# The S5 output products of a decoder trunk: one burst a round over four column groups, in place of four separate calls

## The reference

```
lam_bar = exp(lam * dt)
bu    = einsum('blgh,gph->blgp', ug, b_bar)          # complex
state = linear_scan(broadcast(lam_bar), bu)          # over the 256 tokens
y     = einsum('blgp,ghp->blgh', state, c_c).real + d * ug
```

## Time and profile before

| | |
|---|---|
| median of 3 runs | 2974.36 us (2973.3 to 2975.58) |
| profiled execution, its own time | 2973.05 us |
| its span, first to last instruction | 2971.0 us |
| mean granted TensorE clock | 0.993 |
| TensorE busy | 2894.8 us, 97% |
| VectorE busy | 2010.5 us, 68% |
| ScalarE busy | 1582.0 us, 53% |
| GpSimd busy | 751.4 us, 25% |

### The profile page before, as it was taken

How to read it: one execution, slowest core, us unless ns; L and a number is a source line. 1 busy time by engine, 2 the same in 40 slices (tenths; PEclk the granted TensorE clock), 3 DMA queues, 4 the chain that set the end, 5 groups by cost and what they waited for, 6 DMA issues and landing times.

```text
span 2971.0 us, 56245 instructions
## 1 busy us (share of the span) xinstructions
PE 2894.8 (97%) x16280; PEld 2454.7 (83%) x16280; DVE 2010.5 (68%) x3316; ACT 1582.0 (53%) x2828; POOL 751.4 (25%) x813
## 2 busy tenths in 40 slices
PE   6999999999999999999989999999999999999997
PEld 5878888888888888888877788888888888888886
DVE  7788888755555667555568888887555555665555
ACT  5555554565555655444455554546555655644443
POOL 3145445401000123111123544543000011221110
PEclk9999999999999999999999999999999999999998
DMA  6655555655555556777745555555555555577775
GB/s 225 213 174 159 162 159 154 170 170 168 159 158 164 165 156 195 209 214 209 206 142 174 167 162 159 159 162 171 171 157 164 160 168 154 158 213 209 215 209 176
DMA packets 276414, 522.69 MB, mean 176 GB/s; under 512 B 30912, under 2 KB 33872, under 8 KB 275280
## 3 DMA queue, kind: packets, MB, share of 16 engines
q1 hardware_dynamic: 257360, 477.13, 54.8%
q10 hardware_dynamic: 18944, 44.18, 4.5%
HBM read 508.60 MB, written 16.78 MB: 177 GB/s over the span
## 4 chain that ended last, share of the span: by engine, by line
PE 46%; DVE 2%; issue 2%; ACT 1%; DVEq 0%; POOL 0%; ACTq 0%; POOLq 0%
PE ps L294 26%; PE ps L293 13%; PE ps L443 1%; PE ps L337 1%; DVE w L975 1%; PE ps L456 0%; PE ps L452 0%; PE ps L296 0%; PE ps L325 0%; PE ps L338 0%; DVE zb L1523 0%; PE ps L326 0%; PE ps L327 0%; PE ps L304 0%; PE ps L313 0%
## 5 line engine op out<-in xcount | busy, mean ns | idle before, releaser
L294 PE MATMUL ps<-hb,w 128*128 128x512 f32 x5824 | 2059.1, 396 | 7.3 <-POOL hb L1553 6.1
L975 DVE TENSOR_TENSOR w<-raw,w 128x512 fp32r<-128x512 f32 x1760 | 1290.2, 738 | 859.5 <-ACT w L590 845.1
L590 ACT ACTIVATE w<-raw 128x512 fp32r<-128x512 f32 x1760 | 1098.2, 629 | 1138.6 <-PE ps L294 1135.9
L293 PE MATMUL ps<-hb,w 128*128 128x256 f32 x5690 | 1632.4, 287 | 13.2 <-DVE w L975 11.8
L294 PEld LDWEIGHTS ps<-hb,w 128*128 128x128 f32 x5824 | 1092.9, 188 | 250.5 <-issue 6.7
L293 PEld LDWEIGHTS ps<-hb,w 128*128 128x128 f32 x5690 | 1076.0, 189 | 70.8 <-issue 29.3
L294 PE MATMUL ps<-gl,w 128*128 128x512 f32 x640 | 226.6, 395 | 0.0
L1576 POOL TENSOR_TENSOR xx<-g,tab 128x512 f32<-128x512 f32 x64 | 121.0, 1891 | 269.6 <-DVE g L1038 269.1
L1703 POOL TENSOR_TENSOR nf<-zb 128x256 f32 (+1 forms) x60 | 51.9, 864 | 537.1 <-DVE zb L1491 531.6
L294 PE MATMUL ps<-w,hb 128*128 128x512 f32 x512 | 180.8, 395 | 0.0
L293 PE MATMUL ps<-gl,w 128*128 128x256 f32 x560 | 156.6, 280 | 0.0
(11 more groups left out here) (296 smaller groups left out, 2582.1 us busy)
## 6 DMA issues: line engine op xcount, KB each, us to landing
raw<-in_w SPq DMA_DIRECT2D x1763, 256.0 KB, 2.8
mlaw<-in_mlaw ACTq DMA_DIRECT2D x16, 768.0 KB, 4.2
mlaw<-in_mlaw ACTq DMA_DIRECT2D x16, 512.0 KB, 3.5
gate<-xres ACTq DMA_DIRECT2D x32, 256.0 KB, 4.5
xres<-zb ACTq DMA_DIRECT2D x32, 256.0 KB, 3.7
zb<-in_x SPq DMA_DIRECT2D x8, 512.0 KB, 7.5
xres<-in_x SPq DMA_DIRECT2D x4, 1024.0 KB, 7.0
s5w<-in_s5w ACTq DMA_DIRECT2D x16, 256.0 KB, 3.5
```

Source lines behind the costliest of these rows:

```text
L293: mm(acc[:, T:], a_lo, m_hi, start=False, stop=False, skip_group_check=True)
L294: last = mm(acc, a_hi, m_both, start=(k == 0), stop=(k == nk - 1), skip_group_check=True)
L590: A(w2[:, d, :, 0, :], raw[:, s, :, :], ACT.Copy).then_inc(hi_ready, 1)
L975: V.tensor_tensor(w2[:, d, :, 1, :], raw[:, s, :, :], w2[:, d, :, 0, :].bitcast(F), ALU.subtract).then_inc(w2_ready, 1)
```

## The change

The four calls of `s5_out` in a round become one, at the place where the call for j = 3 was. It goes over the four column groups first with the real parts and then with the imaginary parts. So that all four states are still there, each j has its own tile: `xx`, `kv`, `lg` and `gab`, which joins `ga` and `gb` in one tile of the same total size. `state_used` counts rounds and no longer steps, and GpSimd waits for it once a round.

```diff
-        ga = sb("ga", [P, T])
-        gb = sb("gb", [P, T])
+        gab = sb("gab", [P, 2, T])
+        ga, gb = gab[:, 0, :], gab[:, 1, :]
...
+        states = (xx, kv, lg, gab)
...
-            def s5_out(it, j):
-
-                if j == 0:
-                    pe.wait_ge(cprime_ready, it + 1)
-                    pe.wait_ge(s5_done, it + 1)
-                pe.wait_ge(state_ready, it * 4 + (j + 2))
-                o = ps[32 * j:32 * j + 32, B_Y, 0:T]
-                mm(o, cprime[:, 0, j, :], xx[:, 0, :], start=True, stop=False)
-                mm(o, cprime[:, 1, j, :], xx[:, 1, :], start=False, stop=True).then_inc(state_used, 1)
+            def s5_out(it):
+
+                pe.wait_ge(cprime_ready, it + 1)
+                pe.wait_ge(s5_done, it + 1)
+                pe.wait_ge(state_ready, it * 4 + 5)
+                for a in range(2):
+                    for j in range(4):
+                        last = mm(ps[32 * j:32 * j + 32, B_Y, 0:T], cprime[:, a, j, :], states[j][:, a, :],
+                                  start=(a == 0), stop=(a == 1), skip_group_check=True)
+                last.then_inc(state_used, 1)
...
-                steps = {5: lambda: s5_in(it, 1), 9: lambda: s5_out(it, 0), 13: lambda: s5_in(it, 2),
-                         17: lambda: s5_out(it, 1), 21: lambda: s5_in(it, 3), 25: lambda: s5_out(it, 2)}
+                steps = {5: lambda: s5_in(it, 1), 13: lambda: s5_in(it, 2), 21: lambda: s5_in(it, 3)}
                 if not first:
-                    steps[1] = lambda: s5_out(it - 1, 3)
+                    steps[1] = lambda: s5_out(it - 1)
...
-                V.tensor_tensor(xx[:, :, :], xx[:, :, :], yy[:, :, :], ALU.add).then_inc(state_ready, 1)
+                V.tensor_tensor(states[j][:, :, :], states[j][:, :, :], yy[:, :, :], ALU.add).then_inc(state_ready, 1)
...
-                dve.wait_ge(state_used, it * 4 + 5)
+                dve.wait_ge(state_used, it + 2)
...
-                pool.wait_ge(state_used, it * 4 + (j + 1))
-                G.tensor_tensor(xx[:, :, :], g2[:, :, :], tab[:, 0:1, :].to_broadcast([P, 2, T]),
+                if j == 0:
+                    pool.wait_ge(state_used, it + 1)
+                G.tensor_tensor(states[j][:, :, :], g2[:, :, :], tab[:, 0:1, :].to_broadcast([P, 2, T]),
                                 ALU.mult).then_inc(back_ready, 1)
...
-                pool.wait_ge(state_used, it * 4 + 1)
+                pool.wait_ge(state_used, it + 1)
```

More of the change, by code:

```diff
@@ L405, in _ @@
                 steps = s5_steps(l * G8 + 7, more=False)
-                steps.update({3: k_turn, 6: k_sum, 33: lambda: s5_out(l * G8 + 7, 3), 46: latent_columns,
+                steps.update({3: k_turn, 6: k_sum, 33: lambda: s5_out(l * G8 + 7), 46: latent_columns,
                               50: lambda: spread([ps[:, B_B, 0:T], ps[:, B_B, T:]], c_l + 2), 70: glu_columns,
```

## The result

The changed kernel takes 2922.56 us (median of 4, 2919.06 to 2923.53) against 2974.97 us on the same chip: 52.4 us less, ratio 0.9822 with a 95% interval of 0.9805 to 0.9839. I had predicted 2945 us with 2925 as the lower end: the direction was right, the gain was 1.78 times the forecast 29.4 us and the time lay just outside the range.

A forecast was written before the change was run, and what follows sets the result against it. TensorE was taken to bound twelve of sixteen S5 rounds, with VectorE taking part of the saving in four. 33.6 us saved in the bursts less 4.2 lost early gave 29.4, so 2945 us from a 2974.36 median; range 2925 to 2967.

The forecast's parts named there:

- parts 6 and 7: GpSimd's waits and the state tiles: dropped waits bring nothing, a delay of 1.4 us is covered, the tiles cost nothing.
- parts 3 and 5: Burst after chunk 1 of the next round: TensorE waits no longer there; VectorE's `s5_tail` behind it adds no cost.
- rival D: TensorE gains, but VectorE stalls of 2 us in each round take it back: 2971 to 2977 us; chance 0.05.
- rival A: Products never stream side by side, only shape changes saved: 3.65 us a round, 9.4 us less, 2965 to 2966; chance 0.24.
- part 2: New order of the 16 passes over four column groups in a round: saves between 9.4 and 50.7 us in all.
- 9 slots: Burst's 16 passes, overlapping in issue order, take 2.14 us: 2.10 less a round, 33.6 us in all; chance 0.52.
- 4 slots: Burst's passes spread over all four column groups, 1.07 us: 3.17 less a round, 50.7 us in all.
- rival B: All four column groups abreast: 50.7 us less 6.3 lost in early rounds, 2930 us, or 2924 without loss; chance 0.11.
- change of shape: TensorE going into and out of the 32-column shape: 0.18 us a call, three saved a round, 8.6 us in all.
- serial burst: One burst a round with the array working on one product at a time: 3.65 us in place of 4.24, 0.59 less.
- loss in the early rounds: First two rounds of each layer: VectorE takes back half the saving, 4.2 us, with bounds 0 and 8.4.
- Rival C: Each change of column group in the burst costs 0.11 or 0.164 us: kernel slower, 2977 or 2983 us; chance 0.08.

The follow-up runs named there:

- four tiles alone: The kernel before with only the four state tiles, the four calls left in place and GpSimd waiting once a round: 2971.93 us, ratio 1.0005.
- group-by-group run: The changed kernel with the burst's eight products ordered column group by column group, real then imaginary part of each: 2924.71 us, ratio 0.9843.

## Why the prediction was wrong

**What held.** TensorE bounds the S5 rounds and every microsecond taken from its stream there came off the time: 3.46 us a round on TensorE and 3.46 us a round in length. The tiles and the dropped waits of GpSimd cost nothing (parts 6 and 7, four tiles alone), and neither the burst's later place nor the tail behind it stalls TensorE in the steady rounds, where it is busy all the time (parts 3 and 5). VectorE at 86% was forecast and 87% measured at a larger saving, and rival D (VectorE takes it back) has no wait in the steady rounds to show for it. The serial sum of rival A, 3.65 us, came out once the products were put in one group.

**The step that failed** is part 2, the 9 slots. I wrote that "the two passes of one product still can't" lie side by side, which is right, and took the products "in the order in which they were issued", which is not. I let pass one of group 1 wait until pass two of group 0 could start beside it. The records and the group-by-group run show no such order between groups: a pass waits for its own group only, and the next group's passes go ahead of it. That makes the 4 slots of rival B, to which I had given 0.11 with the argument that "the two passes of a product stand next to each other in the stream". This was worth 17.1 us (50.7 - 33.6) of the 20.5 by which the 49.9 us of the spans exceed my 29.4.

**Mis-sized terms.** A change of shape costs 0.28 us and not 0.18: I took the cost of a call up to the first large product behind it, while the pair that starts there is itself 0.10 us slow. Three calls fewer in 16 rounds make that 3 x 0.10 x 16 = 4.8 us. Against the 0.59 a round that I gave to a serial burst stand 0.84 measured. The loss in the early rounds was 5.6 us in the profile, near the 4.2 of my sum (6.3 for rival B), but that nearness is partly luck: other profiles put it as low as 2.2. Its place is rather round 0 of each layer, in its half with one-tile chunks, than both first rounds evenly, and I had not read that half. Together 50.7 + 4.8 = 55.5, less 5.6, is 49.9, the difference of the spans.

**The rest of the difference** to the medians, 52.4 against 49.9 us, is which executions were profiled: that of before, 2973.05 us, lies 1.9 us below its median, that of the changed kernel, 2922.87, lies 0.3 above, and 0.3 us are outside the spans.

**The two rules.** That products in different column tiles run concurrently (the Trainium skill, "TensorE: Matmul & The Clock Gate", Part 3) agrees with the trace: four groups start within 0.03 us. The same page of the Trainium skill also says that products are strictly first in, first out. The group-by-group run does not agree, if each f32 product is counted as the two passes that the records show: passes of later products start at 231.44 to 231.46, before the second pass of the first at 231.66. The same page of the Trainium skill says, as my prediction has it, that loads overlap with running products only where the row group differs. The trace does not agree with that either: the load at 285.36 runs under the stream that began at 285.33 on the same rows, and the four groups go from pass to pass every 0.21 to 0.24 us. Rival C, which rested on it or on a drained array, asked for gaps of 0.11 or 0.164 us between groups; they are 0.01.

**The waits in round 0, and what is left open.** TensorE's longest wait for `w` there is 3.0 or 1.3 us, and the traces say with what it goes: with whether GpSimd's half of the back rotation for j = 2 takes 3.46 or 1.64 us, behind which ScalarE makes the tables and only then the weights. Holding GpSimd back did not help, as its operation ended just as late; moving the tables cut the wait to 1.49 us and saved no time. Why one execution stretches GpSimd's half and the next VectorE's stays open. So does what limits round 0 once this wait is short: that it is the work of splitting per half-size chunk is argued and not shown by a run of its own.

## What to carry to other kernels

Small products that use a part of the array's rows or columns are worth collecting: here four calls in different 32-column groups cost as much as one, two in different 32-row groups as well, and the order among the column groups did not matter. Read the cost of a small call from the last large product before it to the second one behind it, not the first. When a run takes a suspected cause away, look whether the event that the others wait for really comes earlier. Before a saving is counted for every round, look for rounds whose shape differs; there another engine may already be the limit.

## What the runs showed of the hardware

- f32 products in four column groups stream in the time of one (1.08 us for eight products, 1.06 for two in one group), also when the program has them group by group (1.10 us). In one group the eight take 3.65 us. Two row groups into two PSUM banks do the same (0.99 us for twelve products, 0.98 to 0.99 for six).
- Going into and out of a small shape costs TensorE 0.28 us: 0.08 on the way in, 0.10 on the way out and 0.10 in the first pair of large products after it.
- Where GpSimd's and VectorE's halves of the back rotation overlap, one of them is stretched and not always the same: in the kernel before GpSimd starts at 167.09 and VectorE at 167.51 and they take 1.64 and 1.77 us; at 178.89 and 179.31, the same 0.42 us apart, they take 3.46 and 0.68. Held apart, VectorE's takes 0.68 us and GpSimd's 1.60 to 1.67 in most steps (2.2 to 2.3 in three).
